# A decoder step with mixture of experts: routing in pieces, row columns copied by GpSimd, the last experts' step added by TensorE

## The reference, cut to what matters

```python
xp = layer_norm(alpha * xp + mix, ln1_g, ln1_b)
xp = layer_norm(alpha * xp + moe_ffn(xp, ...), ln2_g, ln2_b)

def moe_ffn(x, w_router, b_router, w_gate, w_up, w_down):
    aff = sigmoid(xt @ w_router)                       # 16 experts in 4 groups of 4
    grp = (aff + b_router).reshape(n_tok, 4, 4)
    g_sel = argmax(sum(top_k(grp, 2)[0], -1), -1)      # one group by the sum of its best two
    _, loc = top_k(in_grp, 2)                          # two experts of that group
    wts = aff of the two / their sum
    h = silu(xs @ w_gate[e]) * (xs @ w_up[e])          # rows sorted by expert
    out = (h @ w_down[e]) * wts                        # added to the row's own token
```

## Time and profile before

| | us |
|---|---|
| runs (three) | 2157.81, 2160.06, 2162.39 |
| median | 2160.06 |
| profiled execution, own time | 2162.91 |
| its span | 2161.1 |
| PE / DVE / ACT / POOL busy | 1928.6 / 1072.7 / 868.1 / 464.7 |

### The profile page before, as it was taken

One profiled execution on the slowest core, in us unless ns is written; L12 is line 12 of the kernel. 1 busy time (PEld: TensorE's weight loads), 2 busy tenths in 40 slices (PEclk: granted clock), 3 DMA queues, 4 the chain that ended last, 5 costly groups with the idle time before them and its releaser, 6 DMA issues. The chain is left out here.

```text
span 2161.1 us, 31196 instructions
## 1 busy us (share of the span) xinstructions
PE 1928.6 (89%) x11491; PEld 1724.1 (80%) x11492; DVE 1072.7 (50%) x1519; ACT 868.1 (40%) x1450; POOL 464.7 (22%) x640
## 2 busy tenths in 40 slices
PE   7989999999999978888888988899986998999981
PEld 6869999999989868777777877798865877788761
DVE  4443212102012457767766777744556575555644
ACT  3002211112110456766766676611013555545643
POOL 0000000000000234444444443200101333333323
PEclk9989999999999969999999999999987999999995
DMA  5011111132213300000000000334234797876955
GB/s 205 1 30 42 47 41 49 40 133 69 81 45 80 118 10 1 1 1 1 1 1 1 2 1 1 108 98 139 88 128 156 249 370 235 291 259 207 336 150 186
DMA packets 100868, 216.22 MB, mean 100 GB/s; under 512 B 25354, under 2 KB 74034, under 8 KB 94578
## 3 DMA queue, kind: packets, MB, share of 16 engines
q1 hardware_dynamic: 90946, 188.90, 24.4%
q0 software_dynamic: 9808, 25.74, 5.2%
HBM read 181.88 MB, written 34.78 MB: 100 GB/s over the span
## 5 line engine op out<-in xcount | busy, mean ns | idle before, releaser
L1569 DVE TENSOR_TENSOR turned_low<-ps,turned_high 128x512 fp32r<-128x512 f32 (+2 forms) x304 | 186.7, 617 | 84.5 <-ACT turned_high L1646 80.9
L1440 PE MATMUL ps<-key_stacks,query_stacks 128*128 128x256 f32 (+3 forms) x384 | 144.4, 376 | 53.2 <-ACT small L1626 27.6
L1646 ACT CAST turned_high<-ps 128x512 fp32r<-128x512 f32 (+2 forms) x304 | 156.9, 526 | 78.7 <-PE ps L1465 78.3
L1545 DVE TENSOR_REDUCE small<-ps 128x1 f32<-128x640 f32 (+7 forms) x256 | 178.0, 696 | 15.6 <-PE ps L1432 14.9
L1699 POOL TENSOR_SCALAR region_w<-region_w,small,gates 128x640 f32<-128x640 f32 (+7 forms) x172 | 133.4, 786 | 226.3 <-DVE small L1549 226.3
L1486 PE MATMUL ps<-turned_high,value_stacks 128*128 128x256 f32 (+1 forms) x608 | 159.6, 296 | 12.0 <-DVE region L1577 11.4
L1635 ACT ACTIVATE region_w<-ps,small 128x640 f32<-128x640 f32 (+7 forms) x172 | 120.5, 701 | 72.3 <-DVE small L1545 65.0
L1486 PE MATMUL ps<-turned_low,value_stacks 128*128 128x256 f32 (+1 forms) x608 | 148.9, 288 | 0.0
L2232 PE MATMUL ps<-down_parts,hidden_parts 128*128 128x512 f32 x576 | 143.9, 407 | 3.0 <-DVE hidden_parts L2500 1.4
L2232 PE MATMUL ps<-gate_parts,rows_parts 128*128 128x512 f32 x576 | 139.1, 397 | 4.8 <-DVE rows_parts L2489 4.8
L1440 PEld LDWEIGHTS ps<-key_stacks,query_stacks 128*128 128x128 f32 x384 | 73.8, 192 | 77.8 <-issue 73.5
(11 more groups left out here) (428 smaller groups left out, 4968.4 us busy)
## 6 DMA issues: line engine op xcount, KB each, us to landing
region_k<-in_w_gate SPq DMA_DIRECT2D x16, 2048.0 KB
region_k<-in_w_up SPq DMA_DIRECT2D x16, 2048.0 KB
region_w<-in_w_down SPq DMA_DIRECT2D x16, 2048.0 KB, 12.8
region_w<-in_w_in SPq DMA_DIRECT2D x20, 512.0 KB, 3.8
gate_b<-region_w SPq DMA_DIRECT2D x8, 516.0 KB, 4.0
region_w<-gate_b SPq DMA_DIRECT2D x8, 516.0 KB, 3.9
region_k<-in_x_prompt SPq DMA_DIRECT2D x8, 512.0 KB, 6.5
region_w<-in_w_in SPq DMA_DIRECT2D x4, 1024.0 KB, 14.2
```

What stands on the lines that cost most here:

```text
L1440: nc.tensor.matmul(out, qs[:, g, tile], k1[:, a, g, k0:k0 + w], start=True, stop=False, skip_group_check=True)
L1545: nc.vector.tensor_reduce(nmax[:, n % 4:n % 4 + 1], sc, AX.X, ALU.max, negate=True).then_inc(s_max, 1)
L1569: nc.vector.tensor_tensor(lo, m.ps[:, turn_bank(G), 0:w], hi, ALU.subtract).then_inc(s_lo, 1)
L1646: nc.scalar.copy(hi, m.ps[:, turn_bank(G), 0:w]).then_inc(s_hi, 1)
```

## The change

- `choose` works by ranks: for each expert how many of its group beat it (a [.., 4, 4] comparison). It runs in `output_and_router`, for tiles 0 to 6 on DVE ahead of tile 8's residual, and for tiles 7 and 8 at the block's end. `route(6)` moves into the products of tile 8. `settle` takes the place of `normalise`: two fused wide passes where there were three. Gate and up weights of expert 0 are loaded behind the store of tile 6.
- The chosen pairs are a bf16 tile ordered by expert. `count` uses bf16. `place_first` and `find_first` find the 128 rows of step 0 (those of expert 0) from the counts alone, and their gather goes out first. `find_rows` moves behind `gate(0)` on PE, `low(GATE, 0)` and `rows_low(0)` move ahead on DVE, `low(UP, 0)` stands ahead of `weigh_pairs`.
- The columns `row_in`, `row_out` and `row_weight` are copied by GpSimd `tensor_copy`, not by DMAs; POOL's order becomes pick, gather, place(s-3), store(s-3).
- The last step is not stored. The sums are loaded when the last but one store has landed. PE adds, in PSUM, an identity product of each tile's sums (float32) and a one-hot product with the last step's result in two parts (fp32r). The second layer norm reads PSUM, in the same block; gain and bias are loaded ahead of the loop.

The diff, cut to its core (helper allocations, semaphores and the removed functions are left out):

```diff
+def choose(nc, dve, m, rs, first, end):
+
+    def step(ins):
+
+        rs.choices += 1
+        ins.then_inc(rs.s_choice, 1)
+        dve.wait_ge(rs.s_choice, rs.choices)
...
+    step(tt(rs.grp[:, cols].rearrange("p (t e) -> p t e", e=NE), m.aff[:, first:end, :],
+            rs.bias.unsqueeze(1).to_broadcast([P, n, NE]), ALU.add))
+    step(tt(ties, other, mine, ALU.is_equal))
+    step(tt(ties, ties, lower, ALU.mult))
+    step(tt(beats, other, mine, ALU.is_gt))
+    step(tt(beats, beats, ties, ALU.add))
+    step(red(rank, beats, AX.X, ALU.add))
+    step(ts(top, rank, 2.0, None, ALU.is_lt))
+    step(tt(kept, grp, top, ALU.mult))
+    step(red(rs.gs[:, groups], kept, AX.X, ALU.add))
...
+    if end == NT9:
+        last = rs.goh[:, TT * NG:NT9 * NG]
+        step(ts(last, last, rs.rowmask, None, ALU.mult))
+    wide = rs.goh[:, groups].unsqueeze(2).to_broadcast([P, n * NG, EPG])
+    for c in range(2):
+        nc.vector.scalar_tensor_tensor(out=by_group(rs.oh[:, c * NQ:(c + 1) * NQ]), in0=rank, scalar=float(c), in1=wide,
+                                       op0=ALU.is_equal, op1=ALU.mult).then_inc(rs.s_choice, 1)
+    rs.choices += 2
+    out = rs.chosen_b.rearrange("p (e t) -> p t e", t=NT9)[:, first:end, :].rearrange("p t (g q) -> p t g q", q=EPG)
+    step(tt(out, rs.top[:, cols].rearrange("p (t g q) -> p t g q", g=NG, q=EPG),
+            goh.unsqueeze(3).to_broadcast([P, n, NG, EPG]), ALU.mult))
...
                 sp.wait_ge(s_x1, t + 1)
                 for rows in (m.x1_dram, m.sum_dram):
                     sp.dma_start(rows[span(t), :], x1[t]).then_inc(m.sem_x1, 16)
+                if t == TT - 2:
+                    sp.wait_ge(s_yl, NT9)
+                    load_third(m, io, sp, GATE, 0)
+                    load_third(m, io, sp, UP, 0)
...
                 for k in range(KT):
+                    if t == TT and k == 2:
+                        route(t - 2)
...
-                if t >= 2:
+                if 2 <= t < TT:
                     route(t - 2)
...
+            def settle(t):
+
...
+                nc.vector.bn_aggr(mv[0:n], stats[0:n, 0:12]).then_inc(s_mv, 1)
+                dve.wait_ge(s_mv, t + 1)
+                stt(out=x, in0=x, scalar=mv[0:n, 0:1], in1=gain[0:n], op0=ALU.subtract, op1=ALU.mult).then_inc(s_norm, 1)
+                dve.wait_ge(s_norm, t + 1)
+                dve.wait_ge(s_rstd, t + 1)
+                stt(out=x, in0=x, scalar=rstd[0:n], in1=bias[0:n], op0=ALU.mult, op1=ALU.add).then_inc(s_x1, 1)
...
+                if t == TT:
+                    dve.wait_ge(rs.s_bias, 16)
+                    dve.wait_ge(rs.s_consts, 1)
+                    dve.wait_ge(s_aff, TT - 1)
+                    choose(nc, dve, m, rs, 0, TT - 1)
...
-                normalise(nc, dve, x1[t], n, stats, mv, rstd, gain, bias, s_stat, s_mv, s_rstd, s_norm, t, s_x1)
+                settle(t)
+            dve.wait_ge(s_aff, NT9)
+            choose(nc, dve, m, rs, TT - 1, NT9)
...
+    z = [m.RK[0:rows_of(t), t * DM:(t + 1) * DM] for t in range(TT)] + [m.small[0:NB, 0:DM]]
+    total_of = [m.R[0:rows_of(t), 8192 + t * DM:8192 + (t + 1) * DM] for t in range(NT9)]
+    out = [m.R[0:rows_of(t), 17408 + t * DM:17408 + (t + 1) * DM] for t in range(NT9)]
+    lanes_last = m.parts("last_lanes", m.at_R, NT9 * P).rearrange("p (t x) -> p t x", x=P)
+    y_last = m.parts("last_out_parts", m.at_RW + 4 * 4096, 2 * DM).rearrange("p (h c) -> p h c", h=2)
...
-            load_third(m, io, sp, GATE, 0)
-            load_third(m, io, sp, UP, 0)
             sp.wait_ge(m.sem_x1, 16 * 2 * NT9)
             load_third(m, io, sp, DOWN, 0)
+            sp.dma_start(gain, io["ln2_g"].rearrange("l d -> (l d)").partition_broadcast(P)).then_inc(s_c, 16)
+            sp.dma_start(bias, io["ln2_b"].rearrange("l d -> (l d)").partition_broadcast(P)).then_inc(s_c, 16)
...
+            sp.wait_ge(s_lo[GATE], 2 * NE)
+            sp.wait_ge(s_lo[UP], 2 * NE)
+            n = steps_of(sp)
+            sp.wait_ge(m.sem_stored, 16 * n)
+            for t in range(NT9):
+                sp.dma_start(z[t], m.sum_dram[span(t), :]).then_inc(s_z[t], 16)
...
-                after(pool, s_t, s)
+                pool.wait_ge(s_t, s)
                 if not isinstance(s, int):
-                    pool.wait_ge(s_mark_in, s - 2)
+                    pool.wait_ge(s_gc, s - 3)
+                    pool.wait_ge(s_mark_in, s - 3)
...
+            def pick(s):
+
+                pool.wait_ge(s_x, 16 * s)
+                nc.gpsimd.tensor_copy(m.row_in[:], m.rows_in[:, bass.ds(s, 1)]).then_inc(s_gc, 1)
+
             def place(s):
 
                 after(pool, s_y, s)
                 pool.wait_ge(m.sem_stored, 16 * s + 16)
                 for dst, src in ((m.row_out[:], m.rows_out), (m.row_weight[:], weights)):
-                    nc.gpsimd.dma_start(dst, src[:, bass.ds(s, 1)]).then_inc(s_oc, 16)
+                    nc.gpsimd.tensor_copy(dst, src[:, bass.ds(s, 1)]).then_inc(s_oc, 1)
 
             def store(s):
-                pool.wait_ge(s_oc, 32 * s + 32)
+                pool.wait_ge(s_oc, 2 * s + 2)
...
+            pool.wait_ge(s_row0, 1)
+            nc.gpsimd.indirect_dma_start(
+                out=xg, out_offset=None, in_=m.x1_dram,
+                in_offset=bass.IndirectOffsetOnAxis(ap=m.row_first[:], axis=0)).then_inc(s_x, 16)
             pool.wait_ge(s_rows, 2)
-            for s in range(3):
+            for s in (1, 2):
                 gather(s, m.rows_in[:, s:s + 1])
             pool.wait_ge(s_weights, 1)
             place(0)
             pool.wait_ge(s_table, 1)
             n = steps_of(pool)
-            with pool.Fori(3, n) as s:
-                pool.wait_ge(s_x, 16 * s)
-                nc.gpsimd.dma_start(m.row_in[:], m.rows_in[:, bass.ds(s, 1)]).then_inc(s_gc, 16)
-                pool.wait_ge(s_gc, 16 * s - 32)
+            last_but_two, last_but_one, last_one = last_three(pool)
+            nc.gpsimd.tensor_copy(row_last, m.rows_out[:, bass.ds(last_one, 1)]).then_inc(s_last, 1)
+            nc.gpsimd.tensor_copy(weight_last, weights[:, bass.ds(last_one, 1)]).then_inc(s_last, 1)
+            gather(3, m.rows_in[:, 3:4])
+            store(0)
+            with pool.Fori(4, n) as s:
+                pick(s)
                 gather(s, m.row_in[:])
+                place(s - 3)
                 store(s - 3)
-                place(s - 2)
-            last_but_two, last_but_one, last_one = last_three(pool)
-            store(last_but_two)
-            place(last_but_one)
-            store(last_but_one)
-            place(last_one)
-            store(last_one)
-            pool.wait_ge(m.sem_stored, 16 * n + 16)
+            for s in (last_but_two, last_but_one):
+                place(s)
+                store(s)
...
             def count():
-                pe.wait_ge(s_m, 1)
-                nc.tensor.matmul(m.ps[:, 0, 0:NQ], rs.before, M, start=True, stop=True)
-                nc.tensor.matmul(m.ps[:, 1, 0:NQ], rs.ones, M, start=True, stop=True).then_inc(s_cnt, 1)
+                nc.tensor.matmul(m.ps[:, 0, 0:NQ], rs.before_b, rs.chosen_b, start=True, stop=True)
+                nc.tensor.matmul(m.ps[:, 1, 0:NQ], rs.ones_b, rs.chosen_b, start=True, stop=True).then_inc(s_cnt, 1)
+
+            def find_first():
+                pe.wait_ge(s_lanes0, 1)
+                for t in range(NT9):
+                    last = nc.tensor.matmul(m.ps[:, 6, 0:2], lanes0[:, t, :], rs.token_b[:, t, :],
+                                            start=(t == 0), stop=(t == TT))
+                last.then_inc(s_found0, 1)
...
+            def down_last():
+                pe.wait_ge(s_lo[DOWN], 2 * NE)
+                pe.wait_ge(s_hl, n)
+                pe.wait_ge(s_y, last_one)
+                for c in range(2):
+                    products(m.ps[:, 5 + c, :], hT, wd, FT, slice(c * 512, (c + 1) * 512)).then_inc(s_dlast, 1)
+
+            def total_rows(t):
+
+                k, b = rows_of(t), 2 * (t % 4)
+                pe.wait_ge(s_z[t], 16)
+                if t >= 4:
+                    pe.wait_ge(s_sq, t - 3)
+                for c in range(2):
+                    nc.tensor.matmul(m.ps[0:k, b + c, :], m.ident[0:k, 0:k], z[t][:, c * 512:(c + 1) * 512],
+                                     start=True, stop=False)
+
+            def add_last(t):
+                k, b = rows_of(t), 2 * (t % 4)
+                if t == 0:
+                    pe.wait_ge(s_onehot, 1)
+                    pe.wait_ge(s_ylo, 2)
+                for c in range(2):
+                    for h in range(2):
+                        last = nc.tensor.matmul(m.ps[0:k, b + c, :], lanes_last[:, t, 0:k],
+                                                y_last[:, h, c * 512:(c + 1) * 512], start=False, stop=(h == 1))
+                last.then_inc(s_added, 1)
+
             count()
-            find_rows()
+            find_first()
             turn_rows(0)
             gate(0)
+            find_rows()
             find_weights()
...
```

(89 more changed lines are left out.)

209 lines of the change are left out of this document (90 added, 119 removed).

## The result

The changed kernel takes **2125.8 us** (median of 4 runs, 2124.4 to 2132.2) against 2161.2 for the kernel before on the same chip: ratio 0.984, 95% interval [0.982, 0.987], some 35 us faster. The forecast was 2134 us, range 2119 to 2151: the time lies in the range, 8 us under the forecast.

A forecast was written before the change was run, and what follows sets the result against it. The loop was taken as near PE's bound, with chains leaving PE idle at both ends; +5.7 - 22.3 - 9.9 = -26.5 us gave 2136.4 against the profiled execution, 2134 us against the median, range 2119 to 2151.

The forecast's parts named there:

- The way into the loop: Ahead of the loop: gate(0) 9.7 us earlier, but up(0) ends at 1665.7 instead of 1660.0, so +5.7 us.
- all warm +1.4: Ahead of the loop: low end of the +5.7 us term, with PE's products all at full clock; all cold +9.
- The loop: gate(1) to gate(23): PE's 18.2 us of gather waits and the low clock go; -22.3 us, bounds -10 and -30.
- the 8 us that I left of the 30.3: In the loop: 8 of 30.3 us lost stay, for store waits, weight and row loads and DVE's halves.
- The copies: In POOL's loop step: three GpSimd column copies cost 0.6 to 6.9 us, the median taken, with POOL time to spare.
- The end: After gate(23): last down product 0.8 us earlier, last stage at PE's 2.79 us a tile; -9.9 us with the 0.8.
- rival C: Last stage: PE at 1.2 GHz, nine tiles at 5.58 us, total 2159 us, about no change; chance 0.06.
- B: In the loop: DMA becomes the bound, loop gain only 10 us, total 2146 us; chance 0.20.
- D: In the loop: store landing, copies, keep, mark and store set the cadence; slower, 2175 us at 20 us steps; chance 0.05.
- E: Better than forecast: the loop's loss goes whole and early gate(0) keeps its clock; 2122 us; chance 0.07.

The follow-up runs named there:

- e6: The changed kernel without the early rows of step 0, engine orders ahead of the loop as in the kernel before; 2113.5 us, ratio 0.979.
- a2: The changed kernel run once more, unaltered, as base for other runs on the same chip; 2124.7 us, ratio 0.981.
- e3: The kernel before with both GpSimd column copies and POOL's new order, nothing else of the change; 2129.6 us, ratio 0.983.
- e1: The kernel before with only the three columns per step copied by GpSimd, POOL's order old; 2146.8 us, ratio 0.993.
- e2: The kernel before with only POOL's new order (pick, gather, place, store), columns still by DMA; 2221.6 us, ratio 1.026.
- e7: The kernel before with POOL's order pick, place(s-3), gather, store(s-3), columns still by DMA; 2145.6 us, ratio 0.992.

## Why the prediction was right

**The way into the loop** (+5.7; measured +2.0). The form was right: gate(0) far earlier, then all of it and more given back behind an idle PE. From gate(0)'s start to up(0)'s end I had 30.3 us and it was 29.7 (14.9 before), with `find_weights` at 4.05 behind an idle of 8.69. Off was the part ahead of it: gate(0) came 12.8 us earlier than before, not 9.7, counted from tile 7. `choose` ended 0.9 us sooner than worked out, the nine small products took 0.40 us where I had 2.0 by those of the earlier trace rows (float32r, 32 columns, cold), and so DVE came to `place_pairs` sooner. The gather itself was slower than forecast: 8.75 us from `row_first` to turned rows, not 6.6, so that the turned rows' copy on ACT ended at 1636.10 and DVE's `place_pairs` at 1636.12: the two chains, of which I had named the second, end together. e6 shows what the forecast only argued: take the early rows out, and gate(1) is 6 us earlier. That 30.3 came so near is in part luck: gate(0) took 7.04 us where I had 8.4, up(0) 8.18 where I had 7.0 (a2: 8.48, 7.32, and 30.3 in all). And the low end, "all warm +1.4", holds gate(0) at the 7.45 of the earlier trace rows; with 5.7 for it the same sum gives -0.3.

**The loop** (-22.3; measured -27.8). The mechanism was right and one term mis-sized: the 8 us that I left of the 30.3 for landings, loads and DVE's halves. It was 2.4, of which 1.6 is gate(1) itself at the lower clock (7.31 against 5.72). In a2 it was 0 (390.28), and in e3 too. Stores landed in 12.7 us and gathers in 9.1 in the median (before: 7.9 and 5.3), and still nothing waited for them long: once the gather is issued in the step ahead, 17.74 us cover it. I had taken the high DMA share of the earlier trace rows for a cost to come; at 287 GB/s in the mean it showed only in waits of ACT of under 3 us each. The stores' longer landing goes with the copies and not with the order: 12.0 us in e1 and 11.6 in e3, 6.3 in e2 and 6.9 in e7; why is open.

One reading behind the forecast was half right: that the small DMAs are late because weight loads fill the engines. In the kernel before `row_in` and `row_weight` landed in 1.7 us in the median, and some 41 of ACT's 97.6 us lie ahead of the issue of `row_weight`, 34 of them while `place` waits for the store to land.

**The copies** (0.6 to 6.9 us of POOL's step; taken: the median, no cost). `row_out` and `row_weight` took 0.19 and 0.18 us in the median, 2.1 and 2.3 at most, and `row_in` 0.37, at most 1.9. What moved is the little mark ahead of the gather: its median went from 0.19 to 1.21 us, since it now comes right behind the turned rows, where DVE often subtracts the gate weights. Of its 20 instructions the 7 with no such subtraction beside them took 0.19 us, the 13 with one 0.30 to 2.31. The Trainium skill (SBUF — State Buffer, Who interferes with whom) says that a DVE instruction with both inputs in SBUF contends with a GpSimd instruction that reads SBUF. The trace agrees: those subtractions take both inputs from SBUF, and beside `rows_low`, which takes one from PSUM, the copies of `row_out` and `row_weight` took 0.17 to 0.20 us. Only 8 of these 46 copies met a subtraction of weights and took 1.31 to 2.25. What made `row_in` take 0.78 us four times with DVE idle is open.

**The end** (-0.8 and -9.1; measured -1.3 and -8.8). Pace 2.65 us a tile against 2.79 worked out, clock 0.99, so rival C is out. From the last down product's end to the last output issued it is 33.9 us (34.1 worked out).

**Rivals.** B (DMA the bound) and D (the chain store, copies, keep) did not come: POOL waited 37.4 us in all for stores, 4.9 at the longest. E's whole loop gain came nearly true, without its clock ahead of the loop: with 2122 it lies nearer to the measured time than the forecast does. What I had not among the rivals is in e2: that the new order without the copies is a large loss. The prediction priced the copies as the removal of waits; they are what makes this order possible.

## What to carry to other kernels

When an edit is a pair (an order and a way of moving data), price each half without the other: here the halves alone are -16 and +59 us, and together -33. Then look at the order of one queue: moving the small DMAs from behind the gather to ahead of it was worth 76 us (e2 to e7). Work brought forward pays only if what *follows* it comes forward as well: here a product came 8 us earlier, its successors stood in DVE's line behind it, PE idled 8.69 us in between and went on at the low clock, and the gain was more than paid back. The best of these kernels by its medians is the changed one without its early rows: 2113.5 us beside a2's 2124.7, and 2116.0 in the repetition. The intervals of the ratios (0.974 to 0.984, and 0.976 to 0.987 for a2) overlap; the 6 to 7 us inside the traces are the firmer number.
